# Row gathers of a mixture-of-experts kernel with 96 indices and 96 partitions in place of 128

## The reference

```
def hier_moe(x, wg, bg, we, be, w_gate_up, w_down):
    ...
    gsel = jnp.argmax(lg, axis=-1)                      # one group of four for each token
    ...
    topv, topi = lax.top_k(le_sel, MOE_TOP_K)           # two experts in it
    ...
    hu = jnp.einsum('td,edf->tef', xt, w_gate_up)       # 2048 -> 2 x 512 for each expert
    hg, hv = jnp.split(hu, 2, axis=-1)
    act = jax.nn.silu(hg) * hv * gates[..., None].astype(x.dtype)
    out = jnp.einsum('tef,efd->td', act, w_down)        # 512 -> 2048

def run_trunk(...):
    for i in range(DEPTH):
        ...
        x = layer_norm(DEEPNORM_ALPHA * x + mix, ln_g[i, 0], ln_b[i, 0])
        ffn = hier_moe(x, ...)
        x = layer_norm(DEEPNORM_ALPHA * x + ffn, ln_g[i, 1], ln_b[i, 1])
```

## Time and profile before

| | us |
|---|---|
| median of three runs | 1452.7 |
| the three runs | 1447.3, 1452.7, 1453.26 |
| profiled execution, its own time | 1448.16 |
| its span, first to last instruction | 1446.1 |
| TensorE busy in the span | 1371.0 |
| GpSimd busy in the span | 28.8 |
| mean granted TensorE clock | 0.983 |

### The profile page before, as it was taken

The page is one execution under the profiler, slowest core; times in us unless marked ns, Lnnn a source line. Parts: engine busy times, 40 slices in busy tenths (PEclk is TensorE's granted clock), DMA queues, the critical chain, the costliest instruction groups (busy, mean ns, idle before and its releaser), DMA issues.

```text
span 1446.1 us, 20719 instructions
## 1 busy us (share of the span) xinstructions
PE 1371.0 (95%) x9012; PEld 757.6 (52%) x9012; DVE 522.7 (36%) x1081; ACT 365.6 (25%) x564; POOL 28.8 (2%) x38
## 2 busy tenths in 40 slices
PE   8999999999899999999898998899999999889895
PEld 8999999999643333343233336653343233224231
DVE  6877887643332021022002118624133013102303
ACT  5667666332310120021012003321021012001101
POOL 0000001000000000000000000000000000000000
PEclk9999999999899999999999999999999999999998
DMA  9775453844599999999999988689999999999993
GB/s 305 229 226 175 152 169 104 277 155 165 203 378 392 427 388 430 427 427 428 427 426 428 426 345 318 220 281 377 426 427 428 427 427 427 426 426 428 426 428 125
DMA packets 94566, 489.03 MB, mean 338 GB/s; under 512 B 8408, under 2 KB 64664, under 8 KB 67320
## 3 DMA queue, kind: packets, MB, share of 16 engines
q1 hardware_dynamic: 89536, 468.61, 81.4%
q10 hardware_dynamic: 2266, 10.27, 2.3%
q0 software_dynamic: 2672, 8.82, 1.6%
HBM read 481.95 MB, written 16.04 MB: 344 GB/s over the span
## 4 chain that ended last, share of the span: by engine, by line
PE 76%; DMA 15%; DVE 5%; ACT 2%; issue 2%; DVEq 0%; POOL 0%; SPq 0%; ACTq 0%; POOLq 0%
PE ps L1260 22%; PE ps L1281 21%; DMA ring<-in_moe_w_down 13%; PE ps L1179 5%; PE ps L1028 5%; PE ps L1030 5%; PE ps L1029 5%; PE ps L1116 2%; PE ps L1118 2%; PE ps L1117 2%; PE ps L1203 2%; PE ps L1344 1%; DMA ring<-in_lru_w_in 1%; ACT xtok L668 1%; DVE xsel L1979 1%
## 5 line engine op out<-in xcount | busy, mean ns | idle before, releaser
L1260 PE MATMUL ps<-ring,xsel 128*64 128x512 f32 x2016 | 455.0, 600 | 16.8 <-DMA ring<-in_moe_w_gate_up 15.8
L1281 PE MATMUL ps<-ring,work 128*32 128x512 f32 x3072 | 346.2, 595 | 9.9 <-DMA ring<-in_moe_w_down 9.9
L1260 PEld LDWEIGHTS ps<-ring,xsel 128*64 128x64 f32 x2016 | 138.2, 137 | 298.9 <-issue 264.0
L1281 PEld LDWEIGHTS ps<-ring,work 128*32 128x32 f32 x3072 | 91.6, 109 | 221.4 <-issue 201.4
L1873 DVE SCALAR_TENSOR_TENSOR arena<-arena,ps 64x512 f32<-64x512 f32 x32 | 21.7, 678 | 479.5 <-ACT work L881 479.5
L1028 PE MATMUL ps<-operands,whi 128*128 128x288 f32 x512 | 152.6, 298 | 0.9 <-DVE ring_lo L1429 0.9
L1030 PE MATMUL ps<-operands,ring_lo 128*128 128x288 f32 x512 | 152.2, 297 | 0.0
L1029 PE MATMUL ps<-ring_lo,whi 128*128 128x288 f32 x512 | 151.5, 296 | 0.0
L1419 DVE TENSOR_TENSOR ring_lo<-ring,whi 128x1024 fp32r<-128x1024 f32 x96 | 115.9, 1222 | 58.9 <-ACT whi L684 58.6
L684 ACT ACTIVATE whi<-ring 128x1024 fp32r<-128x1024 f32 x96 | 100.6, 1058 | 129.0 <-PE ps L1030 71.1
L880 ACT ACTIVATE arena<-ps 64x512 f32<-64x512 f32 x32 | 18.9, 589 | 385.9 <-PE ps L1260 385.9
(11 more groups left out here) (360 smaller groups left out, 1170.7 us busy)
## 6 DMA issues: line engine op xcount, KB each, us to landing
ring<-in_moe_w_gate_up SPq DMA_DIRECT2D x126, 2048.0 KB, 18.8
ring<-in_moe_w_down SPq DMA_DIRECT2D x64, 2048.0 KB, 19.1
ring<-in_lru_w_in SPq DMA_DIRECT2D x15, 2048.0 KB, 10.2
ring<-in_lru_w_out SPq DMA_DIRECT2D x8, 2048.0 KB, 11.9
x_rows<-xtok ACTq DMA_DIRECT2D x4, 1024.0 KB, 3.9
xtok<-in_moe_w_gate_up SPq DMA_DIRECT2D x2, 2048.0 KB, 13.7
ring<-in_pool_w SPq DMA_DIRECT2D x4, 1024.0 KB, 13.5
xtok<-in_x_prompt SPq DMA_DIRECT2D x2, 1024.0 KB, 7.8
```

Of the source, the lines that this page charges most:

```text
L1260: last = mm(ps[half * ES:(half + 1) * ES, e % 2, :], xsel[:, k, e * ES:(e + 1) * ES], wt[:, half * 512:(half + 1) * 512], start=(k == 0), ...
L1281: last = mm(ps[rows:rows + QB, 2 + r, :], act[:, e % 2, f * W + slots0:f * W + slots0 + QB], wt[:, d * 512:(d + 1) * 512], start=start, st ...
```

## The change

The fetch takes its indices from the first 96 partitions of `src_now` and writes the first 96 partitions of `xtok`. The tables, the windows, the waits and the other instructions are as before; on no engine does an instruction change its place, and on GpSimd the ten fetches are the same instructions with 96 x 2048 in place of 128 x 2048.

```
@@ -582,7 +582,7 @@
                 def fetch(turn):
                     eng.wait_ge(x_out[l], 48)
                     eng.wait_ge(src_ready[l], turn)
-                    eng.indirect_dma_start(xtok[:, 0, :], None, x_rows[l], bass.IndirectOffsetOnAxis(src_now[:, 0:1], 0),
+                    eng.indirect_dma_start(xtok[0:W, 0, :], None, x_rows[l], bass.IndirectOffsetOnAxis(src_now[0:W, 0:1], 0),
                                            bounds_check=T - 1, oob_is_err=False).then_inc(rows_in[l], 16)
```

## The result

The changed kernel took 1462.8 us in the median of six runs (1457.91 to 1465.76), the kernel before 1453.0 (six runs). The medians differ by 9.9 us. The ratio is 1.0075, 95% interval 1.0057 to 1.0094: 11 us slower. The prediction had said 1446.5, with a range to 1456.0, and had given 0.05 to slower. The profiled execution of the changed kernel has a span of 1463.7 us, and its own time, 1465.8 us, is the highest of its runs.

What follows compares the result with a forecast made beforehand. The DMA engines were taken to set the pace in windows 1 and 2 of each layer. 3.07 + 0.42 + 0.67 = 4.2 us gained took 1448.16 to 1444.0; forecast 1446.5, midway between run levels, range 1441.3 to 1456.

Steps and rivals of the forecast that it cites:

- The stretches that DMA sets the pace of: About 520 to 726.87 and 1005 to 1288.66, windows 1 and 2 of each layer: DMA time there is paid for.
- a dropped index is a packet without bytes: In the fetches on GpSimd's queue: a dropped index makes a packet but moves no row, 9 ns each.
- 2352 packets: GpSimd's queue after the change: 2672 - 320 packets, with the same 8.82 MB.
- the paced fetches: Five fetches in DMA-paced stretches: fullest engine goes from 8 rows to 6, 0.61 us each, 3.07 us gained; chance 0.5.
- a window of 122 us: 604.90 to 726.87: 120.6 us if spread evenly, 122.1 with 8 + 6 rows on the fullest engine; measured 122.0.
- the slower side: Fetches on fewer engines, 12 rows for 8: 1.23 us more each, 8.6 us in all, own time 1456.8; chance 0.1.
- The first fetches: Each layer's first fetch lands 0.67 us sooner; 0.42 counts in layer 0, 0.67 in layer 1. Alone, as rival: chance 0.2.
- The slack: Layer 0, 510 to 520: loads had caught up, share 0.80, so the fetch at 443.33 saves nothing.
- wrong altogether: Sign against the prediction: a change in the first 384 us or in window 3, where nothing that changes is waited for.

Runs made afterwards that it cites:

- Experiment 8: Kernel before, but the eleven scatters take 128 indices and read 128 partitions, the last 32 dropped, where they took 96; 1452.7 us, ratio 1.0021.
- experiment 1: Changed kernel's 96-index fetches, each with a second fetch of 32 out-of-bounds indices into partitions 96 to 127; 1463.6 us, ratio 1.0089 to the kernel before.
- experiment 3: Kernel before, but fetches take 112 indices and write 112 partitions; 1465.4 us, ratio 1.0095.
- experiment 5: Kernel before plus a plain transfer of 96 rows of 8192 bytes to 96 partitions ahead of the fetches of windows 0 to 2, each layer; ratio 1.0194.
- experiment 6: Kernel before plus a plain transfer of 128 rows of 6144 bytes to 128 partitions ahead of the fetches of windows 0 to 2, each layer; ratio 1.0090.
- experiment 7: Kernel before plus a transfer of 96 rows of 8192 bytes to the device's memory ahead of the fetches of windows 0 to 2, each layer; ratio 1.0084.
- Experiment 4: Kernel before, with its six plain loads of a normalisation row going to 128 partitions instead of 96; 1448.6 us, ratio 0.9986.
- experiment 10: Kernel before, but only the first fetch of each layer takes 96 indices; 1450.5 us, ratio 0.9994.
- experiment 2: Kernel before, each fetch split in two, 64 indices to partitions 0 to 63 and 32 to 64 to 95; 1468.5 us, ratio 1.0123.
- experiment 9: Kernel before plus a plain transfer ahead of the fetches of windows 0 to 2, to 64 or 32 partitions; 1470.8 and 1458.6 us, one run each.

## Why the prediction was wrong

**Right.** The stretches that DMA sets the pace of, with five of the ten fetches in them; that a dropped index is a packet without bytes; 2352 packets; that the change acts in the transfer of those fetches' rows, while GpSimd's 0.05 us mean nothing. These were the places where the time then changed, with the other sign.

**The step that failed** is the one of the paced fetches: "with 96 partitions in 16 blocks an engine has 6", and so "I take two rows, 0.61 us, off the fullest engine for each fetch", 5 x 0.61 = 3.07 us gained. It counted rows for an engine as if an engine's speed didn't depend on where it writes. The runs put a loss of 2.1 to 2.8 us for each such fetch in its place, 12.2 us for the five by the table above, against 11 us in the ratio.

That the fullest engine sets the pace had only one witness, a window of 122 us where even spreading was to give 120.6. That sum left bytes out: 52.14 MB were moved between the landings, not 51.5 (the ring's loads were 50.81 MB, the rows 1.23, the queue of instructions 0.10), and at 428 GB/s they take 121.8 us without any engine being fuller than another. Experiment 8, with up to eight rows for six on an engine in each scatter, ran its windows at the same 427 GB/s. So no run shows a gain from two rows fewer; if there is one, it is inside the net figure. Experiments 1, 3 and 5 to 7 show the condition: a transfer that writes on-chip memory in other than 128 partitions, beside loads that write 128. Experiment 4 shows that indirect addressing isn't needed for it, and experiment 10 that the shape alone isn't enough: there must be loads beside it.

**The size.** Where two engines want the same place and each packet takes twice its 0.307 us, a row costs 2 x 0.31 / 16 = 0.039 us of loading. What was missing, over the 20 us behind each of the five transfers in question:

| kernel | partitions | rows in five | missing, us | for a row, us |
|---|---|---|---|---|
| changed kernel | 96 | 385 | 12.2 | 0.032 |
| experiment 1 | 96 (and 32, no rows) | 385 | 12.2 | 0.032 |
| experiment 5 | 96 | 480 | 15.2 | 0.032 |
| experiment 3 | 112 | 385 | 14.2 | 0.037 |
| experiment 2 | 64 and 32 | 385 | 16.9 | 0.044 |
| experiment 9 | 64 | 320 | 13.7 | 0.043 |
| experiment 9 | 32 | 160 | 7.1 | 0.045 |
| experiment 6 | 128 | 640 (of 6144 bytes) | 0.3 | 0.000 |

The missing bytes account for nearly all of the loss: 12.2, 12.2, 14.2 and 16.9 us stand against 11, 13, 14 and 18 us by the ratios of the changed kernel and experiments 1, 3 and 2. With 64 partitions in experiment 9 they and the bytes of the transfers (6.1 us) make 19.8 us of the 20.1 measured; with 32 they make 10.2 where one run measured 7.9. With the same number of partitions the cost goes by rows; a row costs least with 96 partitions and most with 64 and 32. The estimate of 0.039, less the rows in their own block, is in keeping with 96 and 112. It is under what 64 and 32 cost, so two engines that take turns can't be all of it. Nothing here shows which engine wrote where.

The Trainium skill, "DMA: Bandwidth & Descriptors", section "The descriptor swizzle", says that in a 128-partition transfer each engine writes one port of the on-chip memory. I had read that section for how many rows an engine gets (it gives an engine four partitions and, 32 further on, another four, not a block of eight; with 56 rows the fullest has 8 by either), and passed over what it says of ports. If it holds, 128-partition transfers never meet at a port, and others may. Experiments 5 and 6 fit that (283 against 417 GB/s at full share). That it is a port that is shared is argued from this page and not shown, and the costs with 64 partitions fit no division of the transfer that I know of.

**The evidence was there.** The holes of experiment 4 stood in the trace of the kernel before: 257 GB/s at a share of 1.05 from 995 to 1000, while two 96-partition loads were under way. The prediction looked only at the share and at the rate of whole slices. It had in its rivals that a fetch had never been run at 96, and priced the slower side by 12 rows on an engine (1456.8 for its own time); the right question was what else has 96 partitions on the writing side, and at what rate it ran.

**The first fetches.** Two terms, 0.42 and 0.67 us, for a fetch that lands sooner. It didn't: in layer 1 the chain has it, from issue on, for 4.85 us before and

```profile
952.83 4.99 DMA xtok<-x_rows,src_now
```

after, and in experiment 10 the two take 5.16 and 4.72 us, 0.1 less than before and not 0.6. In layer 0 the wait of 0.42 us is gone as forecast, but by chance: the 16 filling matmuls took 6.54 us where they had taken 6.06. They start 3.4 us later than before, and the granted clock leaves 0.50 some 4 us later, at about 391 for 387. The rows' own transfer isn't what the landing waits for there, or not only. What does was not tried.

**The slack.** In layer 0 the fetch of window 0 costs no time in the changed kernel either: from the first fetch to window 1's first product are 134.7 us in both (384.32 to 519.04, 387.69 to 522.39). The loads, which had caught up by 510, have less in hand: at the same distance from the first fetch, 513.4 to 523.4, the share is 0.95 at 405 GB/s, for 0.80 at 328 before.

In layer 1 the slack was used up: the wait that ends at 1059.05 is new, and the stretch from the first fetch to it is 5.9 us longer than the same stretch before. Two holes make it up. The 27 us from 40 us behind the layer's first fetch, ahead of the second one's rows, hold nearly all of the two normalisation loads to 96 partitions; the 33 us after that hold the fetch. The kernel before:

```profile
985.13:1012.13 27.00, 27.00 (x196) 9.11 (x194) 10.28 (x43) 2.00 (x4) 0.00 (x0) 1.00 1.01 357
```

the changed kernel:

```profile
992.83:1019.83 27.00, 27.00 (x196) 9.01 (x194) 7.41 (x41) 2.00 (x4) 0.00 (x0) 1.00 1.01 328
1019.83:1052.83 33.00, 30.43 (x190) 9.53 (x186) 5.94 (x4) 1.67 (x3) 0.96 (x1) 1.00 1.01 393
```

and experiment 7, whose fetches take 128 indices:

```profile
991.14:1018.14 27.00, 27.00 (x194) 9.11 (x194) 7.42 (x41) 2.01 (x4) 0.00 (x0) 1.00 1.01 332
```

The fetch's own part is (427 - 393) x 33 = 1122 KB, 2.6 us. Over the 67 us ahead of it the changed kernel is behind the kernel before by another 2.6 us of bytes, but experiments 6, 7 and 8, with the fetches of the kernel before, are behind by 1.7 to 2.3 us in the same place. So most of this second part isn't the change: the profiled execution of the kernel before was a good one there. Experiment 4, with these loads in 128 partitions, has 421 GB/s in the 27 us.

Behind the last landing (1304.98), in window 3, where a difference was to mean "wrong altogether", the changed kernel takes 1.3 us more than before. Experiments 4 and 10, in which nothing there is changed, take 1.8 and 1.5 us more than the kernel before, so 1.3 us says nothing.

## What to carry to other kernels

Look at share and rate of the DMA engines together: full share at less than the full rate, over 5 us or so, means that transfers hamper each other, and the transfers of other shape under way at that moment are the ones to ask about. Beside a stream of 128-partition loads, make every transfer into on-chip memory 128 partitions wide, even if rows are dropped or written for nothing: the 32 dropped packets cost 9 ns each, their absence 2.1 to 2.8 us. Transfers out of on-chip memory, here the scatters, need no such padding.

## What the runs showed that was not expected

A plain 96-partition load of 0.79 MB beside weight loads costs 3.0 us more than the same bytes in 128 partitions, which make no hole in the rate. 112 partitions are as bad as 96. Two transfers of 64 and 32 are worse than one of 96 (1.0123 against 1.0075), and a row costs most with 64 and 32 partitions, 0.044 us of loading for 0.032 with 96. And the part ahead of any fetch varies by as much as the whole kernel does from run to run: the first fetch was issued between 381.9 and 388.4 us in the thirteen profiles, in which nothing ahead of it was changed but a small tile in some.
